# Heads reordered, stage ends split in pairs, and two weight remainders of the differential output projection made by GpSimd

## The reference, cut to what matters

```python
# cross attention, 4 heads of 256: o = softmax(q k^T / 16) v ; x = x + o @ w_xo
# sparse layer: 16 heads of 64, here every key is in reach of both branches
ps = masked_softmax(ss, ms); o_sel = ps @ vg
o_win = masked_softmax(sw, mw) @ vw_
o = g[..., 0:1] * o_cmp + g[..., 1:2] * o_sel + g[..., 2:3] * o_win
# differential layer: 8 heads, two score maps of 64 each, one value of 128
#   o = (softmax(q1 k1^T) - lam * softmax(q2 k2^T)) v, then an RMS norm of each head, times a gain
#   x = x + g1 * (o @ w_out)
# mlp: x = x + g2 * (square(relu(h @ w_mlp_in)) @ w_mlp_out)
```

## Time and profile before

| | us |
|---|---|
| median of 3 runs | 1334.8 |
| runs | 1330.15 to 1335.09 |
| profiled execution, its own time | 1333.07 |
| its span in the trace | 1331.3 |
| TensorE busy | 1302.8 |
| VectorE, ScalarE, GpSimd busy | 953.3, 657.2, 79.2 |

### The profile page before, as it was taken

The page is one execution under the profiler, slowest core; times in us unless marked ns, Lnnn a source line. Parts: engine busy times, 40 slices in busy tenths (PEclk is TensorE's granted clock), DMA queues, the critical chain, the costliest instruction groups (busy, mean ns, idle before and its releaser), DMA issues.

```text
span 1331.3 us, 24630 instructions
## 1 busy us (share of the span) xinstructions
PE 1302.8 (98%) x10637; PEld 1247.3 (94%) x10637; DVE 953.3 (72%) x1216; ACT 657.2 (49%) x870; POOL 79.2 (6%) x132
## 2 busy tenths in 40 slices
PE   8999999999999999999999999999999999999998
PEld 7999999999899999999998589999999878999998
DVE  5769897764788767676876878878788675754443
ACT  4544536453734433344556647444455454654442
POOL 4013000000000000021000000000000000000000
PEclk9999999999999999999999999999999999999999
DMA  9665545444578778776632056899865421455550
GB/s 274 201 206 187 178 159 190 159 159 151 175 284 301 255 260 279 269 270 191 184 103 89 1 212 215 317 314 317 311 213 167 162 65 60 162 185 180 182 183 33
DMA packets 172701, 259.67 MB, mean 195 GB/s; under 512 B 5157, under 2 KB 147794, under 8 KB 172594
## 3 DMA queue, kind: packets, MB, share of 16 engines
q1 hardware_dynamic: 160906, 203.13, 46.4%
q0 software_dynamic: 10848, 53.69, 11.5%
q10 hardware_dynamic: 840, 1.28, 0.3%
HBM read 257.03 MB, written 1.05 MB: 194 GB/s over the span
## 4 chain that ended last, share of the span: by engine, by line
PE 86%; DVE 9%; ACT 3%; issue 2%; DMA 1%; SPq 0%; ACTq 0%; POOLq 0%; DVEq 0%
PE ring L669 60%; PE acc L669 24%; DVE w_lo L1997 2%; ACT w_hi L1466 1%; DVE arena L2046 1%; PE acc L1270 1%; PE ring L1078 1%; DMA raw<-in_w_in_dram 1%; ACT arena L1466 1%; DMA arena<-in_w_ada_dram 1%; DVE arena L2410 0%; DVE h_lo L2042 0%; ACT h_hi L1466 0%; DVE h_lo L2040 0%; DVE stat L2604 0%
## 5 line engine op out<-in xcount | busy, mean ns | idle before, releaser
L669 PE MATMUL ring<-h_hi,w_hi 128*128 128x256 f32 (+1 forms) x2016 | 575.8, 286 | 5.6 <-DVE w_lo L1997 1.8
L669 PE MATMUL ring<-h_hi,w_lo 128*128 128x256 f32 (+1 forms) x2016 | 569.4, 282 | 0.0
L669 PE MATMUL ring<-h_lo,w_hi 128*128 128x256 f32 (+1 forms) x2016 | 567.7, 282 | 0.0
L1997 DVE TENSOR_TENSOR w_lo<-raw,w_hi 128x2048 fp32r<-128x2048 f32 x191 | 435.4, 2287 | 166.2 <-ACT w_hi L1466 165.6
L1466 ACT ACTIVATE w_hi<-raw 128x2048 fp32r<-128x2048 f32 x191 | 363.2, 1905 | 133.1 <-PE acc L669 63.5
L669 PEld LDWEIGHTS ring<-h_hi,w_hi 128*128 128x128 f32 x2016 | 381.2, 189 | 11.1 <-issue 6.8
L669 PEld LDWEIGHTS ring<-h_lo,w_hi 128*128 128x128 f32 x2016 | 381.9, 189 | 2.6 <-issue 2.2
L669 PEld LDWEIGHTS ring<-h_hi,w_lo 128*128 128x128 f32 x2016 | 382.1, 190 | 0.0
L669 PE MATMUL acc<-e_hi,w_hi 128*128 128x256 f32 x768 | 217.2, 283 | 0.7 <-DVE e_lo L2445 0.4
L669 PE MATMUL acc<-e_lo,w_hi 128*128 128x256 f32 x768 | 215.1, 280 | 0.0
L669 PE MATMUL acc<-e_hi,w_lo 128*128 128x256 f32 x768 | 215.1, 280 | 0.0
(11 more groups left out here) (319 smaller groups left out, 1356.5 us busy)
## 6 DMA issues: line engine op xcount, KB each, us to landing
arena<-in_w_ada_dram POOLq DMA_DIRECT2D x64, 768.0 KB, 6.4
raw<-in_w_mlp_in_dram SPq DMA_DIRECT2D x32, 1024.0 KB, 5.4
raw<-in_w_mlp_out_dram SPq DMA_DIRECT2D x32, 1024.0 KB, 5.0
raw<-in_w_in_dram SPq DMA_DIRECT2D x24, 1024.0 KB, 5.4
raw<-in_w_e_gate_dram SPq DMA_DIRECT2D x16, 1024.0 KB, 6.1
raw<-in_w_e_up_dram SPq DMA_DIRECT2D x16, 1024.0 KB, 5.5
raw<-in_w_e_down_dram SPq DMA_DIRECT2D x16, 1024.0 KB, 5.0
raw<-in_diff_w_in_dram SPq DMA_DIRECT2D x12, 1024.0 KB, 5.6
```

The costliest lines, as they stand in the source:

```text
L669: return nc.tensor.matmul(dst, lhs, rhs, start=start, stop=stop, **kw)
L1997: tt(w_lo[q % RAW][:, 0:n], raw[q % RAW][:, 0:n], w_hi[q % SPL][:, 0:n].bitcast(F32), ALU.subtract)\
```

## The change

- Cross attention: `x_turn(3)` moves ahead of `x_values(2)`, and the first output panel is taken in four pieces of two blocks (`x_o_blocks`), each as soon as a head is ready, between the last turns and values. On ScalarE `x_pt` goes ahead of `x_o_hi`, on VectorE `x_norm` ahead of `x_o_lo`.
- `open_sums` goes; the first matmul on each accumulator bank opens it.
- Sparse heads: VectorE normalises step `u+1` before it copies the turned probabilities of `u`, and the gate's factor is a second scalar of the normalisation instead of an instruction of its own.
- Differential heads: the last value panel is no longer multiplied before the heads but inside steps 0 to 2, in `acc[1]`, in place of filler (`last_values`); ScalarE takes it out after step 2, and `d_values(2)` waits for that. VectorE normalises before it copies, as above. `d_v2` uses two banks, one for each half.
- The `w_lo` of the panels `d_o` and `d_o + 1` is made by GpSimd, behind its last weight loads for the modulation. VectorE skips them, and makes those of `d_o + 2` and `d_o + 3` between the splits of the heads' outputs; ScalarE makes the `w_hi` of these two later too.
- End of the heads: the norm's sums, root and reciprocal are made for the first three pairs and then for the fourth; the first two `d_o` panels are taken together, two blocks at a time, with the fourth pair's spreading in their middle. Filler: 5 becomes 2, 6 becomes 0, 5 becomes 4. The three `stat_pair` calls move back by up to one panel.

```diff
+            for q in (PN["d_o"], PN["d_o"] + 1):
+                pool.wait_ge(S("hi_made"), q + 1)
+                pool.wait_ge(S("panel_split"), q)
+                nc.gpsimd.tensor_tensor(w_lo[q % RAW][:], raw[q % RAW][:], w_hi[q % SPL][:].bitcast(F32), ALU.subtract)\
+                    .then_inc(S("panel_split"), 1)
...
             x_turn(2)
-            keep_busy(t_fill(3), 1)
+            x_o_blocks(0)
+            x_turn(3)
             x_values(2)
-            x_turn(3)
+            x_o_blocks(1)
             x_values(3)
+            x_o_blocks(2)
+            x_o_blocks(3)
...
-            for i in (2, 3):
-                linear_rows(PN["d_v"] + i, d_v_fill(i))
+            linear_rows(PN["d_v"] + 2, d_v_fill(2), halves=True)
...
+                if h == 2:
+                    pe.wait_ge(S("d_o_out"), 1)
...
             for h in range(DIFF_HEADS):
                 if h == 0:
-                    busy_turn(0, 4)
+                    last_values(range(0, 6))
...
                 if h == 0:
-                    busy_turn(h, 5)
+                    last_values(range(6, 12))
...
                     d_values(h - 1)
-                    busy_turn(h + 1, 1)
+                    if h < 3:
+                        last_values(range(2 * h + 10, 2 * h + 12))
+                    else:
+                        busy_turn(h + 1, 1)
...
-            s_sums((0, 1, 2))
+            s_sums("s_sums", (0, 1, 2)).then_inc(S("summed_s_sums"), 1)
             d_values(DIFF_HEADS - 1)
-            keep_busy(FL["s_spread"], 5)
-            s_sums((3,)).then_inc(S("summed_s_sums"), 1)
-            keep_busy(FL["s_spread"], 6)
+            keep_busy(FL["s_spread"], 2)
+            s_sums("s_sums3", (3,)).then_inc(S("summed_s_sums"), 1)
             pe.wait_ge(S("s_table_landed"), 16)
             pe.wait_ge(S("s_inverse"), 1)
-            head_spread(FL["s_spread"], (0, 1, 2, 3), D_HEADS, lambda j: bank(FL["s_spread"] + j), "spread_s_spread")
-            keep_busy(FL["d_o"], 5)
-            linear_first([PN["d_o"]], FL["d_o"], pairs_ready("so_ready"))
+            spread_pairs((0, 1, 2))
+            keep_busy(FL["d_o"], 4)
+            opening((0, 1))
+            opening((2, 3))
+            pe.wait_ge(S("s_inverse"), 2)
+            spread_pairs((3,))
+            opening((4, 5))
+            opening((6, 7))
...
-                step(tt(z, z, n_gates[:, 2 * b:2 * b + 2, 4 * br:4 * br + 2], ALU.mult))
                 for o in range(2):
-                    w = n_p(u, o)
-                    ts(w[:, 0:P], w[:, 0:P], z[:, o, 0:1], None, ALU.mult)
+                    w, g = n_p(u, o), n_gates[:, 2 * b + o, 4 * br:4 * br + 2]
+                    ts(w[:, 0:P], w[:, 0:P], z[:, o, 0:1], g[:, 0:1], ALU.mult, ALU.mult)
```

More of the change, by code:

```diff
@@ L1043, in spread_gates, with down @@
                             last.then_inc(S("gates_spread"), 1)
[L1045 to L1050, removed]
+            def down(p, slot, first_one=False, last_one=False):
                 open_panel(p)
@@ L1102, in expert_step @@
                 pe.wait_ge(S("act_split"), e + 1)
-                down(p + 2, e % 2)
+                down(p + 2, e % 2, first_one=e == 0)
             for e in range(EXPERTS - 1):
@@ L1382, in _, with last_values @@
             head_spread(FL["d_spread"], (4, 5, 6, 7), D_SPREAD, d_spread_bank, "spread_d")
-            for i in (2, 3):
-                linear_rows(PN["d_v"] + i, d_v_fill(i))
+            linear_rows(PN["d_v"] + 2, d_v_fill(2), halves=True)
+            def last_values(steps):
+                p = PN["d_v"] + 3
+                if steps[0] == 0:
+                    open_panel(p)
+                wh = w_hi[p % SPL][:].rearrange("p (k n) -> p k n", k=KB)
+                wl = w_lo[p % RAW][:].rearrange("p (k n) -> p k n", k=KB)
+                for i in steps:
+                    t, k = divmod(i, KB)
+                    o, c = acc[1][:, t * T:(t + 1) * T], slice(t * P, (t + 1) * P)
+                    mm(o, h_hi[:, k, c], wh[:, k, :], k == 0, False, skip_group_check=True)
+                    mm(o, h_hi[:, k, c], wl[:, k, :], False, False, skip_group_check=True)
+                    last = mm(o, h_lo[:, k, c], wh[:, k, :], False, k == KB - 1, skip_group_check=True)
+                if steps[-1] == 2 * KB - 1:
+                    last.then_inc(S("panel_done"), 1)
             def d_scores(h):
@@ L1933, in take_v @@
                 f = d_v_fill(i)
-                func(vals, bank(f)[:].rearrange("p (t n) -> p t n", t=2), ACT.Copy).then_inc(S(f"drained{f % BANKS}"), 1)
+                if i == 3:
+                    func(vals, acc[1][:].rearrange("p (t n) -> p t n", t=2), ACT.Copy).then_inc(S("d_o_out"), 1)
+                elif i == 2:
+                    for t in range(2):
+                        func(vals[:, t], bank(f + t)[:, 0:T], ACT.Copy).then_inc(S(f"drained{(f + t) % BANKS}"), 1)
+                else:
+                    func(vals, bank(f)[:].rearrange("p (t n) -> p t n", t=2), ACT.Copy).then_inc(S(f"drained{f % BANKS}"), 1)
             take_v(0)
@@ L2783, in _ @@
                     drains(last, FL["d_spread"] + j - 4)
-            ahead(PN["d_v"] + 2)
             def d_max(h):
@@ L2816, in _ @@
                     d_max(h + 2)
+                if h + 1 < DIFF_HEADS:
+                    d_norm(h + 1)
                 if h % 2:
```

108 lines of the change are left out of this document (61 added, 47 removed).

## The result

The changed kernel took 1316.46 us (median of 4 runs, 1315.27 to 1317.45), the kernel before 1333.58 beside it. The ratio is 0.9877, interval 0.9857 to 0.9897: 17.1 us faster, with 1316 forecast. The profiled execution took 1315.27, its span 1313.5, so that span against span it is 17.8 us, against 17.25 in the sum.

What follows compares the result with a forecast made beforehand. TensorE, busy 1302.8 of 1331.3 us, was taken as the bound, with gains only in its waits and filler. 2.4 + 4.1 + 0.75 + 5.8 + 5.5 - 1.3 = 17.25 off 1333.07 gave 1316, range 1309 to 1322 (8 in 10).

Steps and rivals of the forecast that it cites:

- the five places: Where TensorE waits or runs filler: cross attention, sparse heads, differential heads, the end of these heads, zero matmuls before an MLP.
- Sparse heads: VectorE's loop falls to 5.7 us in two steps, under TensorE's 6.1; six waits go: gain 4.1, bounds 2.0 and 4.6.
- the idle figures begin where a matmul is modelled to end, ... six times: 1.0: Sparse heads: idle is counted from 0.16 us behind where the next matmul could start, adding 1.0 to the 3.3 of waits.
- copy and product leave it: Sparse heads: copy and gates' product leave the loop TensorE waits for, 0.67 us in each two steps.
- Zero matmuls: Four opening matmuls go: nothing gained before the experts or in the first MLP, gain 0.75 in the second; bounds 0 and 1.5.
- a chain that TensorE doesn't feed: First MLP: VectorE's modulation, for which TensorE waits 1.83 us, so the zero matmuls' gain is lost there 25 us later.
- Last value panel: Its 48 matmuls move from before the differential heads into filler's place, heads keeping their length: gain 5.8.
- Sums to output: Behind the differential heads, first output matmul comes 7.4 us after the sums instead of 12.92: gain 5.5, bounds 4.5 and 6.2.
- Output panels to MLP: Fourth spreading costs 0.35 and the sum before the second MLP waits 1.0: loss 1.3, bounds 0.3 and 4.
- GpSimd: Two remainder subtractions, 3.8 to 10.9 us each, hidden before they are wanted; counted as nothing, up to 3 us at risk.
- Rival 5: GpSimd's subtractions hold VectorE through the differential heads, 0.5 us an instruction: 1332 or above 1335; chance 0.03.
- rival 6: Without nine fillers the clock falls to 1.2 GHz in or behind the differential heads; chance 0.02 of costing 10 us or more.

Runs made afterwards that it cites:

- the order alone: Kernel before with only VectorE's sparse-head order changed, next step's normalisation ahead of the copy: median of 10 runs 1329.54 us, ratio 0.9975.
- the folded product alone: Kernel before with only the gates' product folded into the sparse heads' normalisation, order as before: 1334.31 us over 10 runs, ratio 1.001.

## Why the prediction was right, point by point

**The total**: 17.25 forecast, 17.8 in the trace. That it is so near is luck: 1.2 too much for the sparse heads and 1.7 too little for the first MLP cancel. The mechanism was right in the four large terms.

**What bounds the kernel**: confirmed at the five places. The stretches between them, which carry nothing of the change, kept their length within 0.3 us.

**Cross attention**: 2.7 measured, the upper bound; 2.4 said. No run takes its parts (order, pieces, the swaps on the other engines) one from another.

**Sparse heads**: the mechanism was right (waits gone, TensorE the bound, 6.1 us in two steps), the size was not: 2.9 for 4.1. The step that failed is "the idle figures begin where a matmul is modelled to end, ... six times: 1.0". The waits summed to 3.3 and one of 0.4 is left; the difference is the whole gain, with nothing on top. (The prediction's own terms, 3.3 and 1.0, make 4.3 and not 4.1.) And "copy and product leave it": the product leaves as an instruction and comes back in four longer ones; only the order counts.

**Zero matmuls**: 1.06 in the second MLP (the shift goes from -16.78 to -17.84) for 0.75, and nothing before the experts, as said. In the first MLP the zeros' time (1.05) was lost 13 us later, at the remainder of activations, as the shifts there show (-5.62, -6.67, -5.61). The step that failed is that TensorE waits behind that for "a chain that TensorE doesn't feed". It feeds it by way of the panels that it releases: their loads and the modulation's hold each other up. Taking the zeros out moved a panel's load 1.2 us further ahead of the modulation's, and the wait of 1.83 ended (shift -7.54). With the zeros back, 0.92 of it is back.

**Last value panel**: 5.8 said and measured, the heads' length unchanged (27.70 in both traces). The eleven fillers of 0.43 in the prediction are 4.7 us, not 4.9; nothing rests on it.

**Sums to output**: 5.4 for 5.5. That the chain, not the filler, set the time is shown by less filler in the kernel before: the reciprocal came no earlier. What in the chain gave the gain was not taken apart. Two things changed, and the prediction names both: the first three pairs no longer wait for the fourth, and ScalarE's two `w_hi` no longer stand ahead of the last square (nor VectorE's two `w_lo`, which ended as its reciprocal began). The root that has to wait for that square, before:

```profile
1108.56 0.47 ACT L1466 ACTIVATE norm<-ring,eps 128x256 f32<-128x256 f32 x1 [0.72 <-PE ring L669]
```

and after:

```profile
1093.40 0.47 ACT L1503 ACTIVATE norm<-ring,eps 32x256 f32<-32x256 f32 x1 [0.76 <-PE ring L675]
```

It begins 5.92 us behind the sums before and 3.82 after. So, as an estimate from these two rows, some 2.1 of the 5.4 us would come from moving this work on panels alone, without any split in pairs. No run shows it.

**Output panels to MLP**: 0.6 lost net, 0.55 said, but with other parts. The fourth spreading cost 1.05, three times the 0.35 counted, since the pairs had run side by side; the fourth sum waited only some 0.3 (ScalarE's last square starts at 1126.44, the sum at 1127.11) where 1.0 was counted.

**GpSimd**: 4.6 us each, hidden, no collision. Right for the reason given, but the margin was thin: the second ended when the heads began, and with the two begun 18.3 and 15.6 us later the heads are 8.4 us longer. Rival 5 counted 0.5 us for each instruction that meets GpSimd; what was measured is the rest of the subtraction, 3.3 and 4.3 us, and the clock behind it.

**The filler** (rival 6): 0.02 for a loss of 10 was fair, but its argument, that the busy share "hardly changes", covered only this change. Some filler is needed: away altogether it costs 1.2 us here.

## What to carry to other kernels

Where a chain through other engines sets a stretch, shorten the chain first and take filler away only as far as the stretch shrank; filler alone gives nothing and may cost the clock. A wait of TensorE is also a date for a load: before removing one, look at what its earlier release sends onto the DMA engines beside the loads of another queue. GpSimd is free help only where VectorE is idle or reads PSUM; a small instruction that meets it can wait for all that is left of GpSimd's. And a small group of matmuls that ran beside others does not get cheaper by being taken out of the group.

## What the runs showed of the hardware

- A `tensor_scalar` of VectorE on two fp32 numbers a partition took 3.49 us beside a GpSimd subtraction, 0.23 alone.
- Matmuls of four pairs, each on 32 rows, start within 0.02 us of each other: 16 records take 1.15 us, 12 take 1.14, 4 take 1.12.
- A `tensor_scalar` on 128x128 is 0.06 us longer with two scalars for each partition than with one (343 against 284 ns; 407 against 348 at 128x256).
- Much of the scatter of the runs is one stretch. Behind the small matmuls at 711 the clock is 0.50 for a time that differs from one execution to the next. Over 16 us it was 0.89 in the kernel before and in the changed one. In the profiled execution of the kernel with the order alone, the slowest of its ten, it was less, and so it was in that of the folded product alone (0.68 too):

```profile
708.00:724.00 16.00, 16.00 (x104) 14.37 (x103) 7.37 (x17) 8.15 (x24) 0.00 (x0) 0.68 0.08 27
```

0.21 of 16 us are 3.4 us, more than that edit gives. What decides how long it lasts stays open; nothing was tried on it.
